# Mixer 2 with its heads' scores in pairs and its rows in column halves; the opening's loads and the window bias reordered

## The chip, the cores and the metric

One core of one Trainium2 chip runs the whole program. The metric is device time in microseconds (us) of that core, as the median of the runs shown. A profiled execution is a separate run; its span (first to last instruction) is what the trace divides up.

## What is computed

Two transformer-like blocks of two layers each, on a sequence of 256 tokens (two tiles of 128), width 1024, all in float32. Cut to its order:

```python
for l in range(2):                      # first block
    mod = silu(c) @ w_mod[l] + b_mod[l] # nine vectors of 1024: shifts, scales, gates
    x = x + 0.5 * g1 * swiglu(modulate(x, norm_g[l, 0], sh1, sc1), w_ffn1_gu[l], w_ffn1_down[l])
    x = x + g2 * (mixer_1(modulate(x, norm_g[l, 1], sh2, sc2)) @ w_out[l])
    #   mixer_1: 6 latent heads, 6 window heads with a relative-position bias, 4 stick-breaking heads
    x = x + 0.5 * g3 * swiglu(modulate(x, norm_g[l, 2], sh3, sc3), w_ffn2_gu[l], w_ffn2_down[l])
for l in range(2):                      # second block
    mod = silu(c_2) @ w_ada[l] + b_ada[l]
    q, k, v, g_sw, p_in, gates = split(h @ w_in[l])   # 11 strips of 512 columns
    ret = head_rmsnorm(retention(q, k, v))            # 8 heads, q and k of 64, v of 128
    ret_d = (silu(g_sw) * ret) @ w_ret_o[l]
    pool_d = (group_linear(causal_pool(p_in)) * pool_scale[l]) @ w_pool_o[l]
    merged = sigmoid(a_ret) * ret_d + sigmoid(a_pool) * pool_d
    x = x + g1 * (merged @ w_out[l])
    x = x + g2 * swiglu(modulate_2(rmsnorm(x, norm2[l]), sh2, sc2), w_ffn_in[l], w_ffn_out[l])
return rmsnorm(x, final_norm)
```

In retention, head by head, the scores q·k are multiplied by a fixed decay matrix and then applied to v.

## The kernel before

Each float32 operand is split into a high and a low part, and a product is made of three matmuls (high·high, high·low, low·high), lines 1776 to 1778. Weights stream in units of 128 x 1024. SP (SyncE's queue) loads a unit into one of six raw slots (`RING`), ScalarE writes its high part (`hi_static`, line 677), VectorE its low part (`lo_static`, line 1131), into seven slots (`PARTS`), and TensorE consumes it: 12 matmuls of 512 columns a unit in `strip_unit` and `rows_unit`. Semaphores count units: `w_loaded`, `hi_done`, `lo_done`, `mm_done`.

The order on each engine is written out by hand; nothing reorders it. There are eight phases: ffn, mixer 1, ffn, twice over, then mixer 2, ffn, twice over. Counted by `f`, the feed-forwards are f = 0 to 5; the mixers are m = 0, 1 of each kind.

The opening (lines 452 to 495, 809 to 834, 1333 to 1377, 1930 to 1943): SP loads 16 units of modulation weights (`mod_load`), then strip 0 of the first feed-forward. TensorE sums them (`mod_unit`), makes four of six `bias_pass`es between them, turns x (`x_turn`), and starts on strip 0 (`first_strip`, which wants for column pair u of a token tile both `lo_done` of unit u and `hlo_done`, counted by `x_low`). The rest of the constants, 768 KB, and five small gain vectors are loaded from ScalarE's queue behind the split of x (line 831), and TensorE waits for them before strip 1 (line 1943).

A feed-forward runs through 11 strips (`STRIPS`) of 256 gate and 256 up columns. In round b TensorE makes `gate_up` of strip b (4 units), in the middle of it the `turn` of strip b-1, then `down` of strip b-1 (2 units). VectorE splits weights, makes `gated` and `act_lo`, and adds up modulation units for later phases: `mod_slot(f, b)` says which ones in round b. Those units come through a ring of four slots (`MOD_RING`) that GpSimd's queue fills (line 426), each load waiting for the unit that had the slot. In a chunk of eight units the last is summed on TensorE (`mod_sum`), which also frees its slot.

The window bias is made in six passes: VectorE compares positions (`bias_reach`), TensorE multiplies (`bias_pass`, 64 small matmuls in banks 4 to 7), VectorE reduces (`bias_take`, four reductions). Passes 4 and 5 stand in mixer 1, m = 0, between the units of its second strip; `bias_mask` then applies scale and mask, in part in f = 0, round 3, in part in the mixer.

Mixer 2 (lines 2208 to 2338): strips 0 to 6 give q, k, v, the gate and the pool input; between strips 3 and 4 all four groups of transposes of q and k; after strip 6 the eight heads, one after another. For head i TensorE makes scores i, waits for VectorE's product with the decay, and makes values i-1. A head's q and k lie on partitions 0 to 63 or 64 to 127 by turns. Then strips 7 to 10, four groups of transposes of `ret`, the pooling matmuls, eight row units of `w_ret_o`, four of `w_pool_o`, eight of `w_out` behind `merged(0)` and `merged(1)`, which turn the two column halves of the merged rows. Banks of strips: `STRIP_BANKS`. The pool rows fill all four banks by rows first; only their last two units go by column half, and VectorE's merge of half 0 waits for `pool_half`.

## Time and profile before

| | us |
|---|---|
| median of three runs | 1874.15 |
| lowest, highest | 1869.9, 1875.66 |
| the profiled execution | 1882.45 |
| its span | 1880.6 |
| TensorE busy | 1813.6 (96%) |
| VectorE busy | 1340.4 (71%) |
| ScalarE busy | 920.3 (49%) |
| HBM traffic, mean | 233 GB/s |

Places in the span that are spoken of, in us from its start: opening 0 to 36, feed-forward f = 0 36 to 244, mixer 1 m = 0 244 to 364, m = 1 751 to 863, mixer 2 m = 0 1056 to 1273, m = 1 1474 to 1682. A row of a timeline gives start, length, engine, line, operation, result and operands, count, and in brackets the idle time before it and what ended it. A matmul's length covers its filling; the distance between starts is what it costs. In a table of windows, PEclk is the clock granted to TensorE as a share of its full 2.4 GHz: 1.00 is that level, 0.50 is 1.2 GHz.

### The profile page before, as it was taken

How to read it: one execution, taken by the hardware profiler on the slowest of the kernel's cores; microseconds unless marked ns; L12 is line 12 of the kernel's file. 1: busy time of each engine (PE TensorE's matmuls, PEld its weight loads, DVE VectorE, ACT ScalarE, POOL GpSimd, SP SyncE). 2: the span in 40 equal slices, each digit the busy share in tenths (PEclk: the TensorE clock that was granted, in tenths of full speed). 3: DMA queues.
4: the chain of work that ended last, by engine and by line, in shares of the span. 5: the costliest groups of instructions: out<-in, count | busy, mean ns of one | idle time of the engine just before them, and what ended most of it. 6: DMA issues, size and time to landing. Idle time of an engine off the chain costs nothing.

```text
span 1880.6 us, 24264 instructions
## 1 busy us (share of the span) xinstructions
PE 1813.6 (96%) x9140; PEld 1473.7 (78%) x9140; DVE 1340.4 (71%) x1825; ACT 920.3 (49%) x1507; POOL 177.3 (9%) x359
## 2 busy tenths in 40 slices
PE   6999989999999999999999999999999999999997
PEld 3778779788878887887888787877778787878886
DVE  6778777787878877768788765467777755477454
ACT  4343467743464445766433643446343644454344
POOL 3111010111101111011110000001111000000000
PEclk8999999999999999999999997999999999999999
DMA  9889733498959796517898652457898553456652
GB/s 343 317 306 339 286 101 113 157 318 300 329 207 342 274 339 220 169 46 252 301 331 312 210 198 90 164 177 258 311 343 308 190 189 135 152 188 237 213 201 79
DMA packets 241156, 439.49 MB, mean 234 GB/s; under 512 B 15168, under 2 KB 157328, under 8 KB 240912
## 3 DMA queue, kind: packets, MB, share of 16 engines
q1 hardware_dynamic: 205600, 311.09, 48.7%
q0 software_dynamic: 34016, 122.74, 17.2%
q10 hardware_dynamic: 1424, 4.12, 0.6%
q8 instruction: 72, 1.18, 0.2%
q14 instruction: 44, 0.36, 0.1%
HBM read 436.80 MB, written 1.09 MB: 233 GB/s over the span
## 4 chain that ended last, share of the span: by engine, by line
PE 79%; DVE 10%; DMA 5%; ACT 3%; issue 2%; SPq 0%; DVEq 0%; ACTq 0%
PE bank L1776 24%; PE bank L1778 23%; PE bank L1777 23%; DVE weights_lo L1131 5%; DMA arena<-in_w_mod 1%; PE bank L1966 1%; DMA arena<-in_w_ada 1%; DVE mod_acc L1152 1%; ACT weights_hi L677 1%; DMA weights_raw<-in_w_mod 1%; DVE x L1284 1%; DVE arena L1278 1%; PE bank L2252 1%; PE bank L1843 1%; DMA weights_raw<-in_w_ffn_in 1%
## 5 line engine op out<-in xcount | busy, mean ns | idle before, releaser
L1131 DVE TENSOR_TENSOR weights_lo<-weights_raw,weights_hi 128x1024 fp32r<-128x1024 f32 (+2 forms) x584 | 671.7, 1201 | 144.6 <-ACT weights_hi L677 143.8
L1776 PE MATMUL bank<-weights_hi,hT_hi 128*128 128x512 f32 (+1 forms) x1760 | 697.5, 396 | 16.6 <-DVE hT_lo L1248 6.6
L1778 PE MATMUL bank<-weights_hi,hT_lo 128*128 128x512 f32 (+1 forms) x1760 | 684.9, 389 | 0.0
L1777 PE MATMUL bank<-weights_lo,hT_hi 128*128 128x512 f32 (+1 forms) x1760 | 683.9, 389 | 0.0
L677 ACT ACTIVATE weights_hi<-weights_raw 128x1024 fp32r<-128x1024 f32 (+2 forms) x584 | 567.4, 1037 | 65.8 <-DMA weights_raw<-in_w_ffn_gu 22.1
L1776 PEld LDWEIGHTS bank<-weights_hi,hT_hi 128*128 128x128 f32 x1760 | 331.9, 189 | 87.7 <-DVE hT_lo L1248 6.8
L1778 PEld LDWEIGHTS bank<-weights_hi,hT_lo 128*128 128x128 f32 x1760 | 331.5, 188 | 68.3
L1777 PEld LDWEIGHTS bank<-weights_lo,hT_hi 128*128 128x128 f32 x1760 | 332.3, 189 | 62.5
L858 ACT ACTIVATE actT_hi<-bank 128x512 fp32r<-128x512 f32 x66 | 39.6, 599 | 502.6 <-PE bank L1966 502.6
L1152 DVE SCALAR_TENSOR_TENSOR mod_acc<-arena,silu_cond,mod_acc 128x1024 f32<-128x1024 f32 x184 | 236.2, 1284 | 50.0 <-DMA arena<-in_w_ada 17.5
L1776 PE MATMUL bank<-weights_hi,actT_hi 128*128 128x512 f32 (+2 forms) x552 | 218.0, 395 | 4.4 <-DVE weights_lo L1131 4.2
L1777 PE MATMUL bank<-weights_lo,actT_hi 128*128 128x512 f32 (+2 forms) x552 | 213.2, 386 | 0.0
L1778 PE MATMUL bank<-weights_hi,actT_lo 128*128 128x512 f32 (+2 forms) x552 | 213.1, 386 | 0.0
L1393 DVE TENSOR_TENSOR actT_lo<-bank,actT_hi 128x512 fp32r<-128x512 f32 x66 | 45.5, 690 | 125.3 <-ACT actT_hi L858 125.3
L1776 PEld LDWEIGHTS bank<-weights_hi,actT_hi 128*128 128x128 f32 x552 | 103.6, 188 | 38.4 <-issue 16.1
L1778 PEld LDWEIGHTS bank<-weights_hi,actT_lo 128*128 128x128 f32 x552 | 103.6, 188 | 21.3
L1777 PEld LDWEIGHTS bank<-weights_lo,actT_hi 128*128 128x128 f32 x552 | 103.7, 188 | 19.1
L426 POOL DMA_DIRECT2D arena<-in_w_mod x128 | 68.1, 533 | 419.5 <-DVE mod_acc L1152 221.1
L659 POOL TENSOR_TENSOR x<-x,arena 128x512 f32<-128x512 f32 x10 | 12.8, 1278 | 711.6 <-DVE arena L1278 711.6
L426 POOL DMA_DIRECT2D arena<-in_w_ada x96 | 50.9, 532 | 291.1 <-DVE mod_acc L1152 152.2
L853 ACT ACTIVATE arena<-bank 128x256 f32<-128x256 f32 x132 | 43.4, 381 | 63.2 <-PE bank L1778 63.2
L1388 DVE TENSOR_TENSOR arena<-arena,bank 128x256 f32<-128x256 f32 x132 | 49.3, 415 | 8.4 <-ACT arena L853 8.4
(274 smaller groups left out, 1259.0 us busy)
## 6 DMA issues: line engine op xcount, KB each, us to landing
weights_raw<-in_w_ffn_gu SPq DMA_DIRECT2D x176, 512.0 KB, 5.5
arena<-in_w_mod POOLq DMA_DIRECT2D x128, 512.0 KB, 6.7
weights_raw<-in_w_in SPq DMA_DIRECT2D x104, 512.0 KB, 4.8
arena<-in_w_ada POOLq DMA_DIRECT2D x96, 512.0 KB, 6.6
weights_raw<-in_w_ffn_down SPq DMA_DIRECT2D x88, 512.0 KB, 4.7
weights_raw<-in_w_ffn_in SPq DMA_DIRECT2D x88, 512.0 KB, 5.8
weights_raw<-in_w_ffn_out SPq DMA_DIRECT2D x44, 512.0 KB, 4.8
weights_raw<-in_w_out SPq DMA_DIRECT2D x32, 512.0 KB, 4.4
```

What stands on the lines that cost most here:

```text
L426: eng.dma_start(mod_tile(m), A[name][layer][k * P:(k + 1) * P, col:col + D]).then_inc(S(mod_sem(m)), 16)
L677: nc.scalar.activation(whi[:, n % PARTS, 0:width], raw[:, slot, 0:width], ACT.Copy).then_inc(S("hi_done"), 1)
L853: nc.scalar.activation(sg_t[:, t, :], bank[gu_banks(j)[t]][:, 0:256], ACT.Silu).then_inc(S("silu_done"), 1)
L858: nc.scalar.activation(ahi[:, j % 2].rearrange("p k n -> p (k n)"), bank[ATB][:, :], ACT.Copy)\
L1131: V.tensor_tensor(wlo[:, n % PARTS, 0:width], raw[:, n % RING, 0:width], whi[:, n % PARTS, 0:width].bitcast(F32), ALU.subtract).then_inc(S ...
L1152: V.scalar_tensor_tensor(acc, w, sc, acc, ALU.mult, ALU.add).then_inc(S("mod_used"), 1)
L1278: V.tensor_tensor(xn[:, t, c], bank[2 * t + h][:, :], gate_b[:, c], ALU.mult).then_inc(S("x_gated"), 1)
L1388: ins = V.tensor_tensor(act_t[:, t, :], sg_t[:, t, :], bank[gu_banks(j)[t]][:, 256:512], ALU.mult)
L1393: V.tensor_tensor(alo[:, j % 2].rearrange("p k n -> p (k n)"), bank[ATB][:, :], ahi[:, j % 2].rearrange("p k n -> p (k n)").bitcast(F32), ...
L1776: T.matmul(o, sh, wh, start=start, stop=False)
L1777: T.matmul(o, sh, wl, start=False, stop=False)
L1778: return T.matmul(o, sl, wh, start=False, stop=stop)
```

## The change

- Opening. SP loads 12 modulation units, then the first half of strip 0, then the other four, then the second half. ScalarE and VectorE split units 0 and 1 of it before the last modulation vector is stored; VectorE then splits units 2 and 3 behind `x_low(0)` and `x_low(1)`. The 768 KB of constants and the gains go from ScalarE's queue to SP's, ahead of strip 1; TensorE's wait for them moves into round 1.
- Window bias. Passes 4 and 5 move from mixer 1 into round 1 of f = 0, with buffers and banks 0 to 3 of their own; one mask over all 384 columns in round 3. Round 1 has no modulation units; its 42 are spread over rounds 2 to 10 (4, 5, 5, 4, 5, 5, 4, 5, 5).
- Mixer 2. Two groups of transposes of q and k, half of strip 4, the other two. Scores in pairs over banks 6, 7, 4, 5; the first pair before the last unit of strip 6, values 0 before that strip's copies. Half of the groups of `ret` are turned before strip 10 and go to the feed-forward's tiles. Pool rows go by column half throughout: 4 units of half 0, 3 of half 1, `merged(0)`, the last.

```diff
-    to = [min(len(units), max(4 * e, len(units) * e // 10)) for e in (b - 1, b)]
+    late = 1 if f == 0 else 0
+    to = [min(len(units), max(4 * e, len(units) * e // (10 - late))) for e in (max(b - 1 - late, 0), b - late)]
...
-STRIP_BANKS = [2 * (s % 3) for s in range(7)] + [4, 6, 0, 2]
+STRIP_BANKS = [0, 2, 4, 0, 2, 0, 4, 4, 6, 0, 2]
+STRIP_AFTER = {3: 0, 4: 1, 5: 3, 6: 2, 7: 6}
+SCORE_BANKS = (6, 7, 6, 7, 4, 5, 6, 7)
...
+            for m in range(MOD_AHEAD):
+                mod_load(sp, m)
+            sp.wait_ge(S("mod_read"), 6)
+            gu_strip(RING, phases[0][2]["gu"], 0, (0,))
+            for m in range(MOD_AHEAD, MOD_FIRST_UNITS):
+                mod_load(sp, m)
+            sp.wait_ge(S("mod_summed"), 1)
+            gu_strip(RING, phases[0][2]["gu"], 0, (1,))
...
-                        sp.wait_ge(S("mod_read"), 7)
-                        sp.wait_ge(S("mod_summed"), 1)
-                    gu_strip(n0, a["gu"], 0)
-                    if n0 == RING:
                         sp.wait_ge(S("mod_summed"), 2)
+                        sp.dma_start(con[:, C_FIRST:], A["con"][:, C_FIRST:]).then_inc(S("const_loaded"), 16)
+                        for dst, src in ((gq96[:, 0, :], "mla_q_norm"), (gq96[:, 1, :], "mla_k_norm"),
+                                         (gw64[:, 0, :], "swa_q_norm"), (gw64[:, 1, :], "swa_k_norm"), (sink[:, :], "sinks")):
+                            sp.dma_start(dst, A[src][0].partition_broadcast(P)).then_inc(S("gains_loaded"), 16)
+                    else:
...
                 hi_static(RING, SLOT)
+                hi_static(RING + 1, SLOT)
                 act.wait_ge(S("scale_ready"), 1)
                 x_hi(0)
                 x_hi(1)
...
+                        if s == 11:
+                            split_groups(4, tiles=[ahi[:, 0], ahi[:, 1]])
                         split_strip(s)
                     strip(10)
-                    split_groups(KD)
...
             bias_take(3)
+            lo_static(RING, SLOT)
+            lo_static(RING + 1, SLOT)
...
                         x_low(g)
-                        lo_static(n0 + g, SLOT)
+                        if g < 2:
+                            lo_static(n0 + 2 + g, SLOT)
...
+                    if f == 0:
+                        bias_reach(4)
+                        bias_reach(5)
                     gated(0)
                     for b in range(1, STRIPS):
                         c = n0 + 4 + 6 * (b - 1)
                         units(c + 2, c + 4)
                         mod_units(mod_slot(f, b))
+                        if f == 0 and b == 1:
+                            bias_take(4)
                         act_lo(b - 1)
-                        units(c + 4, c + 8)
+                        units(c + 4, c + 6)
+                        if f == 0 and b == 1:
+                            bias_take(5)
+                        units(c + 6, c + 8)
                         if b == STRIPS - 1 and after is not None:
                             units(end, end + 2)
                         gated(b)
                         if f == 0 and b == 3:
-                            bias_mask(0, 2 * P)
+                            bias_mask(0, 3 * P)
                         for chunk in mod_full(f, b):
                             mod_store(chunk)
...
+                            if s == 7:
+                                if m == 0:
+                                    dve.wait_ge(S("const2_loaded"), 16)
+                                probs(0)
+                                probs(1)
...
+                        if h == 0:
+                            lo_static(n0 + 60, SLOT)
+                        split_groups(KD // 2, banks=TRB_MERGED[2 * h:2 * h + 2], tiles=[(a[:, 0], a[:, 1]) if h == 0 else hT_tiles(w, 4) for a, w in ((ahi, hhi), (alo, hlo))])
+                        if h == 0:
+                            lo_static(n0 + 61, SLOT)
...
                         gate_up(c, 0, 2)
+                        if f == 0 and b == 1:
+                            bias_pass(4)
                         turn(b - 1)
-                        gate_up(c, 2, 4)
+                        gate_up(c, 2, 3)
+                        if f == 0 and b == 1:
+                            bias_pass(5)
+                            pe.wait_ge(S("const_loaded"), 32)
+                        gate_up(c, 3, 4)
+                        if f == 0 and b == 1:
+                            pe.wait_ge(S("bias_taken"), 6)
...
-                        if m == 0 and u in (0, 1):
-                            bias_pass(u + 4)
-                        if u == (2 if m == 0 else 1):
...
+                    def scores(i):
+                        r0 = 64 * (i % 2)
+                        q, k = qkT2[r0:r0 + 64, i // 2, :], qkT2[r0:r0 + 64, 4 + i // 2, :]
+                        b = bank[SCORE_BANKS[i]]
+                        if i >= 4:
+                            pe.wait_ge(S("ret_probs"), RH * m + i - 3)
+                        T.matmul(b[:, 0:SEQ], k[:, 0:P], q, start=True, stop=True)
+                        T.matmul(b[:, SEQ:384], k[:, P:SEQ], q[:, P:SEQ], start=True, stop=True).then_inc(S("ret_scores"), 1)
...
+                    qk_turn(0)
+                    qk_turn(1)
+                    strip(4, 0, 2)
+                    qk_turn(2)
+                    qk_turn(3)
+                    strip(4, 2, 4)
+                    strip(5)
...
+                    scores(0)
+                    scores(1)
+                    strip(6, 3, 4)
+                    copied(5)
+                    values(0)
+                    pe.wait_ge(S("ret_probs"), RH * m + 2)
+                    scores(2)
+                    scores(3)
+                    values(1)
+                    copied(6)
+                    scores(4)
+                    scores(5)
+                    values(2)
+                    values(3)
+                    scores(6)
+                    scores(7)
+                    for h in range(4, RH):
+                        values(h)
+                    for s in range(7, 10):
                         strip(s)
+                    copied(8)
                     pe.wait_ge(S("ret_ready"), m + 1)
-                    copied(8)
-                    transposes(ret, KD)
+                    transposes(ret, 4)
+                    strip(10)
+                    transposes(ret, KD, first=4)
...
-                    for u in range(2):
+
+                    def pool_rows(u, h):
                         n = n0 + 54 + u
-                        rows_unit(n % PARTS, n + 1, u, u == 0, False, hhi, hlo, first_bank=4)
-                    pe.wait_ge(S("lo_done"), n0 + 58)
-                    for h in range(2):
-                        for u in (2, 3):
-                            n = n0 + 54 + u
-                            wh = whi[:, n % PARTS, 512 * h:512 * (h + 1)]
-                            wl = wlo[:, n % PARTS, 512 * h:512 * (h + 1)]
-                            for t in range(NT):
-                                ins = products(bank[4 + 2 * t + h][:, :], u, t, wh, wl, False, u == 3)
                         if h == 0:
+                            pe.wait_ge(S("lo_done"), n + 1)
+                        wh = whi[:, n % PARTS, 512 * h:512 * (h + 1)]
+                        wl = wlo[:, n % PARTS, 512 * h:512 * (h + 1)]
+                        for t in range(NT):
+                            ins = products(bank[4 + 2 * t + h][:, :], u, t, wh, wl, u == 0, u == 3)
+                        if h == 1:
+                            ins.then_inc(S("mm_done"), 1)
+                        elif u == 3:
                             ins.then_inc(S("pool_half"), 1)
-                    ins.then_inc(S("mm_done"), 2)
...
+                    for u in range(4):
+                        pool_rows(u, 0)
+                    for u in range(3):
+                        pool_rows(u, 1)
                     merged(0)
                     split = tr[0] - 1
+                    pool_rows(3, 1)
                     for u in range(5):
...
```

## Rows read from the trace of the kernel before

**Rows 1.** The page's first part: busy us, share of the span, instructions.
```profile
PE 1813.6 (96%) x9140; PEld 1473.7 (78%) x9140; DVE 1340.4 (71%) x1825; ACT 920.3 (49%) x1507; POOL 177.3 (9%) x359
```

**Rows 2.** Waits of TensorE, whole span: us in total, times, longest us.
```profile
PE bank L2006 <- DVE arena L1452: 4.6, 2, 4.4
...
PE bank L2275 <- DVE hT_lo L1262: 2.5, 2, 1.2
...
PE bank L2325 <- DVE arena L1754: 2.1, 2, 1.0
PE bank L1776 <- DVE hT_lo L1262: 2.0, 2, 1.0
...
PE bank L2239 <- DVE arena L1683: 1.0, 2, 0.5
```

**Rows 3.** Timeline of TensorE, first feed-forward: strip 0, strip 1, first turn.
```profile
35.86 0.50 PE L1776 MATMUL bank<-weights_hi,hT_hi 128*128 128x512 f32 x1 [2.41 <-DVE weights_lo L1131]
...
52.45 0.80 PE L1776 MATMUL bank<-weights_hi,hT_hi 128*128 128x512 f32 x1 [4.20 <-DMA con<-in_con]
...
60.73 0.60 PE L1966 MATMUL bank<-con,arena 128*128 128x128 f32 x4
```

**Rows 4.** Windows: us, busy of PE, PEld, DVE, ACT, POOL, PEclk, DMA share, GB/s.
```profile
52.00:54.00 2.00, 1.54 (x4) 1.26 (x5) 1.88 (x3) 0.00 (x0) 0.00 (x0) 0.50 0.56 192
...
1140.00:1160.00 20.00, 20.00 (x69) 16.19 (x68) 5.12 (x15) 0.00 (x0) 0.00 (x0) 0.51 0.00 1
```

**Rows 5.** Timelines of ScalarE and VectorE in the opening.
```profile
36.69 1.04 ACT L677 ACTIVATE weights_hi<-weights_raw 128x1024 fp32r<-128x1024 f32 x1
...
34.24 0.43 DVE L1248 TENSOR_TENSOR hT_lo<-arena,hT_hi 128x256 fp32r<-128x256 f32 x1
```

**Rows 6.** The bias's instructions: duration ns minimum, median, maximum, first and last start.
```profile
L1174 DVE TENSOR_TENSOR arena<-arena x6: 2266/2292/2323, 7.9 to 256.0; 128x2048 bf16<-128x2048 f32 x6
...
L1182 DVE TENSOR_REDUCE window_bias<-bank x24: 442/448/460, 13.4 to 264.6; 128x96 f32<-128x288 f32 x24
```

**Rows 7.** Timelines of VectorE and TensorE, f = 0, round 4.
```profile
118.30 1.28 DVE L1152 SCALAR_TENSOR_TENSOR mod_acc<-arena,silu_cond,mod_acc 128x1024 f32<-128x1024 f32 x1 [4.22 <-DMA arena<-in_w_mod]
...
120.10 4.62 DVE L1131 TENSOR_TENSOR weights_lo<-weights_raw,weights_hi 128x1024 fp32r<-128x1024 f32 x4
...
121.47 0.47 PE L1776 MATMUL bank<-weights_hi,actT_hi 128*128 128x512 f32 x1 [1.87 <-DVE weights_lo L1131]
```

**Rows 8.** Timeline of TensorE, mixer 1: from strip 0 to the gate's turn, both layers.
```profile
243.57 0.47 PE L1776 MATMUL bank<-weights_hi,hT_hi 128*128 128x512 f32 x1 [0.19 <-DVE hT_lo L1248]
...
259.28 0.64 PE L1863 MATMUL bank<-arena 32*128 32x18 bf16 x64
...
277.01 0.27 PE L1888 MATMUL bank<-con,mod_cols 128*8 128x128 f32 x1
...
750.65 0.47 PE L1776 MATMUL bank<-weights_hi,hT_hi 128*128 128x512 f32 x1 [0.18 <-DVE hT_lo L1248]
...
775.54 0.27 PE L1888 MATMUL bank<-con,mod_cols 128*8 128x128 f32 x1
```

**Rows 9.** Timeline of TensorE, mixer 2: scores L2252, values L2260, next strip L1776.
```profile
1137.96 0.71 PE L2252 MATMUL bank<-arena 64*128 64x256 f32 x4 [0.83 <-ACT arena L1061]
...
1139.63 0.49 PE L2260 MATMUL bank<-arena 128*128 128x128 f32 x2 [0.74 <-DVE arena L1695]
...
1160.56 0.57 PE L1776 MATMUL bank<-weights_hi,hT_hi 128*128 128x512 f32 x1
...
1558.41 0.70 PE L2252 MATMUL bank<-arena 64*128 64x256 f32 x2
...
1559.26 0.49 PE L2260 MATMUL bank<-arena 128*128 128x128 f32 x2
...
1568.60 0.49 PE L2260 MATMUL bank<-arena 128*128 128x128 f32 x2
...
1569.29 0.48 PE L1776 MATMUL bank<-weights_hi,hT_hi 128*128 128x512 f32 x1
```

129 lines of the change are left out of this document (52 added, 77 removed).

## The prediction

> **What bounds the kernel now.** I read the page's busy shares first: TensorE is busy 1813.6 of 1880.6 us [rows 1], so it is the bound, and a change can only gain in its 67 us of idleness or where a matmul runs slower than elsewhere. Second, TensorE's waits over the whole span, to name that idleness: each line of them stands in one or two places only, and four recur once per layer of mixer 2 [rows 2]. Third, the granted clock in windows: 1.00 nearly everywhere, but 0.50 behind the wait for the constants and 0.51 for 20.0 us in the heads of mixer 2, m = 0 [rows 4]. Fourth, the same stage in both layers, side by side in the timeline: what the one has and the other hasn't is what can go.
>
> **The base.** The sum is made against the profiled execution: 1882.45 us, a span of 1880.6 and 1.85 around it. That lies 8.3 us above the median, 1874.15. The slow heads of m = 0 cost about 9 us (below), so I suspect that most timed runs lack them. Then part of my gain below exists only against the profiled run. The prediction is that of a run without slow heads, so it needs no correction; if the timed runs had them too, the answer would lie lower by up to 8.
>
> **Opening.** Before, VectorE finishes `x_low(0)` at 34.24 + 0.43 = 34.7 [rows 5] and then splits unit 0, so TensorE starts at 35.86 [rows 3]. With units 0 and 1 split ahead it can start at 34.7. But 1 MB of weights now goes ahead of the last four modulation units; they may land later by up to its own time, and I put 0.5 us on the chain (0 to 1.5). TensorE's second column pair wants `x_low(1)`, and that now stands behind the split of unit 2, whose high part ScalarE makes only after two x groups and a scaling: before that ended at 36.69 + 1.04 = 37.7 [rows 5], with one more unit ahead of it; now about 36.7 + 0.5. Then a split, 4.62/4 = 1.2 [rows 7], and 0.4 for `x_low(1)`: 38.8. So TensorE does one unit (1.4 us), waits 2.3, and finds the rest in about the old order. Strip 0, over at 48.25 before (52.45 less 4.20), is over at about 49.1: **+0.8**. The early units buy nothing.
>
> The wait for the constants goes: **-4.2** [rows 3]. Behind it the clock is at 0.50 [rows 4], and the 24 matmuls from 52.45 to 60.73 take 8.28 us, where 24 at 0.227 take 5.45: **-2.8**. The load isn't cheaper, only needed later: SP issues it at some 32, TensorE asks for it in the middle of round 1, beyond 58. Behind it on SP's queue stand strip 1's loads, later by the six issues, some 3.5 us: they are issued at 35.5 to 38. A load that lands 6 to 9 us later is split by 47.7, before TensorE's 49.1. If that cover were gone each microsecond would count in full.
>
> What the Trainium skill says here: in "Trainium Kernel Development and Optimization", Key Constraints, DMAs from the SP, ACT and POOL queues run on the same 16 engines and interleave, so another queue saves issue time alone. By that the constants still take their share from strip 1's loads wherever they are issued, and nothing is gained from the move in itself; my sum takes no gain from it either.
>
> **Bias passes.** They cost TensorE 0.64 us each [rows 8]: **+1.3** in round 1, in place of the same in mixer 1. VectorE gets 2 x 2.29 and 2 x 4 x 0.45 = 8.2 us [rows 6] instead of four modulation units (4.9). `gated(0)` is queued behind both `bias_reach`es: splits to 48.9, reaches to 53.5, gate to 54.2; TensorE comes to pass 4 at 49.1 + 5.5 = 54.6. Just hidden. `bias_take(5)` stands behind two splits and ends at some 62.6, where TensorE arrives at 61.7: **+0.9**. Sum of opening and round 1: **-4.0**, from -7 (no late landing) to +2.
>
> **Five units a round.** Before, rounds 5 and 10 had five. In round 4 a burst crosses the unit that TensorE sums, needs a fifth slot of a ring of four, and VectorE waits 4.22 us for the load; TensorE then stands 1.87 [rows 7]. Now six rounds have five units, three of them with the crossing. VectorE has slack: six splits 7.2, gate 0.75, `act_lo` 0.7, five units 6.4, together 15.1 of TensorE's 16.8 (six units of 2.73 and a turn). In round 3 the mask stands ahead of the store that round 4's gate turn wants, and round 4's burst starts as late as before with a unit more: 1.3 more. The others I take as hidden to 0.3 each, round 10 as it was: **+1.2**, 0 to +7.
>
> **Mixer 1, m = 0.** From strip 0 to the gate's turn it takes 277.01 - 243.57 = 33.4 us, in m = 1, without bias work, 775.54 - 750.65 = 24.9 [rows 8]. The difference holds both passes, the wait of 4.4 for the latent rows that VectorE makes late (of 4.6 in [rows 2]), and a low clock behind it. What is late next is what is late in m = 1, a wait of 0.2. **-8.5**, -7 to -9.
>
> **Mixer 2.** Three things per layer. (1) The gaps: 0.5 at the q, k transposes (half of strip 4 now hides the copies), 1.25 ahead of the pooling (strip 10 does), 1.05 and 1.0 at `merged(0)` [rows 2]. For the last two: half 0 of the pool rows is now complete after four half units, 5.5 us; VectorE's merge needs 2.5 and is over at 8.1; TensorE has 4.1 us of half 1 and arrives at 9.6. Then 1.4 us of half 1 cover the split of the first group. All four go: **-3.8**.
>
> (2) The heads. In m = 1 strip 7 starts at 1569.29. Scores of one head take 1559.26 - 1558.41 = 0.85, values 0.86 with the change to scores behind them, 0.69 at the end where values or the strip follow. The one pair of scores that stands together takes, in m = 0, 1137.96 to 1139.63 less the wait of 0.74: 0.93, hardly more than one [rows 9]. From the end of strip 6 to the first values it is 2.50 in m = 0 (0.83 of it a wait), and the second scores follow 0.86 on; so in m = 1 strip 6 ended at 1555.05, and the heads take 14.2 us. Now: eight values of 0.69 to 0.86 and four pairs of 0.93, one of them inside strip 6: 9.2 to 10.6, taken 9.9. The waits: VectorE's products take 0.65, between values h-2 and h there are always other values or a pair of 0.7 to 0.9, and the copies of strip 6 are passed by values 0, a pair and values 1. **-4.3**, -3.6 to -5.
>
> (3) The clock. In m = 0 the same stretch takes 1160.56 - 1137.13 = 23.4, at 0.51 [rows 4, 9]; that is 9.2 more than in m = 1, where the instructions are the same. The fall comes just after two waits and among small matmuls. Without the waits and with 4 us less of it, I take it that the clock holds: **-9.2**.
>
> Two layers: -16.2 - 9.2 = -25.4.
>
> **A rule for and against the pairs.** "TensorEngine Tiling (Array Packing)", Key Properties, in the Trainium skill says that tiles on other rows run in parallel, which the 0.93 bears out, and that a change of tiling mode drains TensorE; the trace agrees in so far as values cost 0.86 ahead of scores and 0.69 ahead of their like. By this rule the pairs gain twice, as there are fewer changes; with 0.69 throughout, the heads would be at my lower end.
>
> **Sum.** -4.0 + 1.2 - 8.5 - 25.4 = -36.7; 1882.45 - 36.7 = 1845.7, so **1846 us**.
>
> **Rivals.**
> - The clock falls in the heads of one layer again, in half the runs or more. Against it: no waits left ahead; for it: nothing distinguishes m = 0 from m = 1 now. Some 9.9 us of work at half speed: 1846 + 9 = **1855**.
> - The fifth unit is paid each time: six stalls of 1.9 instead of the 5.3 that I count, +6, and with the unit itself (1.3) +14: **1852 to 1860**, say 1855. For it: [rows 7]; against: bursts that crossed in other rounds were hidden.
> - The pairs don't overlap, because the second waits on something of the first (the change doesn't do what it says): 0.77 for each of eight pairs, +6: **1852**. Against it stands the one pair of [rows 9].
> - The other side: VectorE becomes the bound of the first feed-forward. Its 15.1 us a round and an unhidden wait w for a modulation load, in each of nine rounds, against 16.8. It is slower than before from w = 1.7 + 37/9 = 5.8 us on; now 4.2 was seen once [rows 7]. With heavier traffic, w = 6.5: 9 x 4.8 = 43, **1888**.
>
> **Numbers.** My forecast has 0.60 (its own range 1838 to 1851), the clock 0.15, the fifth unit 0.13, no overlap 0.05, something better than the forecast (timed runs with slow heads before as well) 0.04, the other side 0.03. The range is 1837 to 1859. A measurement of this kernel tells 0.3%, 5.6 us, from no change: faster by more 0.95, within 0.02, slower 0.03.
>
> **What would show it.** In the changed kernel's trace: no wait for the constants, and granted clock 1.00 from strip 0 to round 4; a wait of some 2.3 us ahead of strip 0's second pair; about 0.9 ahead of `down` in round 1; mixer 1's stretch of [rows 8] within 1 us in both layers; none of the last four waits of [rows 2]; strip 6 to strip 7 in 9 to 10 us in both layers at 1.00. I am wrong if the clock is below 1.00 in the heads, if waits of TensorE for line 1131 appear in rounds 3, 6 and 9, or if strip 1 waits for its weights.

## The result and the profile of the changed kernel

The changed kernel takes 1846.32 us (median of four runs, 1843.98 to 1850.63), the kernel before 1874.91 (four runs, 1869.9 to 1876.04): ratio of the means 0.9855, 95% interval 0.983 to 0.9881. The forecast was 1846.0. The profiled execution took 1846.53 us, its span 1844.7, against 1882.45 and 1880.6 before.

TensorE's waits over the whole span, against [rows 2] (total, times, longest):

```profile
...
PE bank L1797 <- DVE hT_lo L1259: 8.8, 20, 2.1
PE bank L1988 <- DVE arena L1402: 5.3, 5, 2.6
...
PE bank L1797 <- DVE weights_lo L1142: 2.5, 3, 1.4
PE bank L1928 <- ACT arena L722: 2.4, 2, 1.3
...
PE bank L1864 <- DVE mod_acc L1163: 1.2, 1, 1.2
PE bank L1911 <- DVE mod_cols L1178: 1.1, 1, 1.1
PE bank L2034 <- DVE arena L1463: 0.4, 2, 0.2
```

The wait for the latent rows (L2034, 4.6 before) is down to 0.4, that for the constants is gone, and so are the four of mixer 2. New are those in the first feed-forward: the gate's turn (L1911), a modulation sum (L1864), and more ahead of the last turns (L1988).

The windows of TensorE, against [rows 4] (us, PE busy, granted clock, DMA share, GB/s):

```profile
20.00:40.00 20.00, 15.27 (x222) 0.67 0.87 303
40.00:60.00 20.00, 18.32 (x142) 1.00 0.91 323
1120.00:1140.00 20.00, 19.89 (x126) 1.00 0.41 138
1420.00:1440.00 20.00, 18.04 (x87) 0.91 0.79 284
```

The heads of mixer 2, m = 0, which stood at 0.51 before, are at 1.00. The low clock behind the constants' wait is gone. The stretch from 20 to 40 us is at 0.67. In the kernel before it had 0.74, with the DMA engines busier:

```profile
20.00:40.00 20.00, 16.47 (x232) 0.74 0.94 325
```

Where the time went, by the ten stages in their order. A stage begins with the first matmul on `hT_hi` behind the transposes of x. I give the kernel before twice, since a second profile of it (e_before, below) looks different:

| stage | before, as profiled | before, again | changed |
|---|---|---|---|
| to mixer 1, m = 0 | 243.57 | 241.25 | 243.45 |
| mixer 1, m = 0 | 118.47 | 118.46 | 108.93 |
| f = 1 | 195.19 | 195.24 | 195.19 |
| f = 2 | 193.42 | 193.41 | 193.43 |
| mixer 1, m = 1 | 110.18 | 109.07 | 108.97 |
| f = 3 | 195.47 | 195.42 | 195.17 |
| mixer 2, m = 0 | 215.32 | 205.90 | 196.85 |
| f = 4 | 202.62 | 206.90 | 205.16 |
| mixer 2, m = 1 | 205.99 | 205.92 | 197.04 |
| f = 5 to the end | 200.37 | 200.53 | 200.51 |
| span | 1880.6 | 1872.1 | 1844.7 |

Three stages carry the gain: mixer 1, m = 0 with 9.5, and mixer 2 with 9.0 and 8.9 (against the second profile; the first has 9.4 us more in mixer 2, m = 0). Between the second profile and the changed kernel lie 27.4 us, between the first and it 35.9. The opening and the first feed-forward together gave nothing: 0.1 against the first profile, and 2.2 longer than the second. The opening in the changed kernel, TensorE and then VectorE, against [rows 3, 5]:

```profile
30.52 1.08 PE L1873 MATMUL bank<-arena,silu_cond 128*32 128x256 f32 x8 [0.63 <-DMA arena<-in_w_mod]
...
41.22 0.47 PE L1797 MATMUL bank<-weights_hi,hT_hi 128*128 128x512 f32 x1 [2.11 <-DVE hT_lo L1259]
43.30 0.47 PE L1797 MATMUL bank<-weights_hi,hT_hi 128*128 128x512 f32 x1 [0.46 <-DVE hT_lo L1259]
...
57.69 0.66 PE L1988 MATMUL bank<-con,arena 128*128 128x128 f32 x4
```

```profile
34.25 0.42 DVE L1174 TENSOR_TENSOR arena<-bank,con 128x256 f32<-128x256 f32 x1 [1.49 <-PE bank L1873]
...
36.90 0.43 DVE L1259 TENSOR_TENSOR hT_lo<-arena,hT_hi 128x256 fp32r<-128x256 f32 x1
39.51 1.23 DVE L1142 TENSOR_TENSOR weights_lo<-weights_raw,weights_hi 128x1024 fp32r<-128x1024 f32 x1 [2.18 <-ACT weights_hi L690]
```

The 2.11 us ahead of the second column pair is there, as it had to be. But VectorE gets the last modulation sum only at 34.25 us, and `x_low(0)` runs at 36.90 where it ran at 34.24 before. The first turn comes at 57.69 instead of 60.73 (58.62 in the second profile of the kernel before).

### The profile page after: what moved, and what is told of

Same layout as the page of the kernel before. It is cut to its first block, busy times and chain, and to the rows that moved or that the text cites. A ratio compares the mean times of both kernels' runs of the same rounds, so it can differ in the third digit from the quotient of the medians.

```text
span 1844.7 us, 24265 instructions
## 1 busy us (share of the span) xinstructions
PE 1788.9 (97%) x9140; PEld 1456.1 (79%) x9140; DVE 1340.6 (73%) x1824; ACT 920.4 (50%) x1507; POOL 176.4 (10%) x359
## 4 chain that ended last, share of the span: by engine, by line
PE 78%; DVE 9%; DMA 7%; ACT 3%; issue 2%; SPq 0%; DVEq 0%; POOL 0%; ACTq 0%
PE bank L1797 24%; PE bank L1799 23%; PE bank L1798 23%; DVE weights_lo L1142 5%; DMA arena<-in_w_mod 2%; PE bank L1988 1%; DMA weights_raw<-in_w_ffn_gu 1%; DMA weights_raw<-in_w_mod 1%; DMA arena<-in_w_ada 1%; DVE mod_acc L1163 1%; ACT weights_hi L690 1%; ACT arena L731 1%; DMA weights_raw<-in_w_ffn_in 1%; DVE x L1295 1%; PE bank L1864 1%
## 5 line engine op out<-in xcount | busy, mean ns | idle before, releaser
L1797 PE MATMUL bank<-weights_hi,hT_hi 128*128 128x512 f32 (+2 forms) x1696 | 669.8, 395 | 10.8 <-DVE hT_lo L1259 8.8
L1799 PE MATMUL bank<-weights_hi,hT_lo 128*128 128x512 f32 (+2 forms) x1696 | 658.3, 388 | 0.0
L1798 PE MATMUL bank<-weights_lo,hT_hi 128*128 128x512 f32 (+2 forms) x1696 | 657.1, 387 | 0.0
L1797 PEld LDWEIGHTS bank<-weights_hi,hT_hi 128*128 128x128 f32 x1696 | 318.5, 188 | 77.8 <-issue 7.3
L1799 PEld LDWEIGHTS bank<-weights_hi,hT_lo 128*128 128x128 f32 x1696 | 318.3, 188 | 65.3
L1798 PEld LDWEIGHTS bank<-weights_lo,hT_hi 128*128 128x128 f32 x1696 | 318.9, 188 | 59.5
L1797 PE MATMUL bank<-weights_hi,actT_hi 128*128 128x512 f32 (+1 forms) x616 | 243.9, 396 | 2.8 <-DVE weights_lo L1142 2.5
L1798 PE MATMUL bank<-weights_lo,actT_hi 128*128 128x512 f32 (+1 forms) x616 | 238.8, 388 | 0.0
L1799 PE MATMUL bank<-weights_hi,actT_lo 128*128 128x512 f32 (+1 forms) x616 | 238.7, 388 | 0.0
L1799 PEld LDWEIGHTS bank<-weights_hi,actT_lo 128*128 128x128 f32 x616 | 116.1, 188 | 24.0
```

What stands on the lines that cost most here:

```text
L1797: T.matmul(o, sh, wh, start=start, stop=False)
L1798: T.matmul(o, sh, wl, start=False, stop=False)
L1799: return T.matmul(o, sl, wh, start=False, stop=stop)
```

## The experiments

Times of different series are not finely comparable: beside my kernels the median of the kernel before lay between 1872.09 and 1874.95 us. I therefore go by the stages of the traces wherever a difference is small.

### Is the slow stretch in the heads always there?

The kernel before, unchanged.

> The kernel before, unchanged, profiled a second time. Theory (the base of the prediction): the half clock in mixer 2's heads of m = 0 belongs to some executions only, so this one shows a granted clock of 1.00 from 1140 to 1160 us with probability of about two in three, and then a span of 1880.6 - 9.2 = about 1871.5 and a time near 1873, the median of the timed runs. Rival A: the half clock stands in every execution at that place (0.50 to 0.55 again, m = 0 some 9 us longer than m = 1) and the profiled run is long for another reason. Rival B: the low clock wanders: m = 0 is at 1.00 and another stage is slow.

Measured: 1873.88 us, span 1872.1. The window that stood at 0.51 in [rows 4]:

```profile
1140.00:1160.00 20.00, 20.00 (x104) 1.00 0.22 64
```

In four series beside my kernels the kernel before ran 48 times: 39 times between 1869.3 and 1877, nine times between 1880 and 1889.3 at a granted clock of 0.982 to 0.989 (4 of 13, 3 of 7, 1 of 17, 1 of 11). The first profile belonged to the second group; of the other nine only the time and the mean clock are known, and that they were slow in the heads too is inferred from these. So the 9.2 us of half clock belong to some executions, as the theory said; if the inference holds, to about one in five.

### Where did the opening's gain go?

e_con is the kernel before with one wait moved:

```diff
                     first_strip(n0, strip_banks, 1)
-                    pe.wait_ge(S("const_loaded"), 32)
...
-                        gate_up(c, 2, 4)
+                        gate_up(c, 2, 3)
+                        if f == 0 and b == 1:
+                            pe.wait_ge(S("const_loaded"), 32)
+                        gate_up(c, 3, 4)
```

> The kernel before with one edit: TensorE's wait for the constants stands in the middle of round 1 of the first feed-forward instead of ahead of it; their load stays on ScalarE's queue. Theory (the prediction's step): the 4.2 us wait goes and the half clock behind it with it, 7.0 us in all: first turn at 60.73 - 7.0 = 53.7 us. Rival: the clock falls there whatever the wait (it is low at 20 to 60 us for the small matmuls of the opening), then 4.2 us alone, first turn at 56.5. Second rival: strip 1's weights are late too and a wait for them takes the place of part of it, first turn at 57 or later.

Measured: 1874.89 us against 1874.95, ratio 0.9999 (0.9972 to 1.0025). The first turn comes at 54.15: 6.6 us earlier than in the first profile of the kernel before, 4.5 earlier than in the second. But one round later (TensorE, then VectorE):

```profile
80.91 0.77 PE L1776 MATMUL bank<-weights_hi,actT_hi 128*128 128x512 f32 x1 [2.91 <-DVE weights_lo L1131]
81.47 0.63 PE L1777 MATMUL bank<-weights_lo,actT_hi 128*128 128x512 f32 x1
81.90 0.63 PE L1778 MATMUL bank<-weights_hi,actT_lo 128*128 128x512 f32 x1
```

```profile
78.28 0.75 DVE L1149 TENSOR_SCALAR mod_acc<-arena,silu_cond 128x1024 f32<-128x1024 f32 x1 [3.12 <-DMA arena<-in_w_mod]
78.95 0.68 DVE L1393 TENSOR_TENSOR actT_lo<-bank,actT_hi 128x512 fp32r<-128x512 f32 x1
79.55 4.62 DVE L1131 TENSOR_TENSOR weights_lo<-weights_raw,weights_hi 128x1024 fp32r<-128x1024 f32 x4
```

VectorE waits 3.12 us for a modulation unit, its splits stand behind that, TensorE waits 2.91, and the clock falls (matmuls 0.43 apart instead of 0.23): this round takes 23.7 us instead of 18.05. Mixer 1 starts at 242.26, between the 243.57 and 241.25 of the two profiles of before. The first theory gave the right size at the first turn, and at the end of the stage nothing of it can be told.

The two medians hide something: in either kernel the executions fall into two groups, and e_con had five of ten in the upper one where the kernel before had four of thirteen. The median of the lower groups is 1871.02 against 1872.82. So up to 1.8 us may have arrived, and the equal medians come in part from the mix.

e_modsfirst is the changed kernel with the opening's order undone:

```diff
-            for m in range(MOD_AHEAD):
-                mod_load(sp, m)
-            sp.wait_ge(S("mod_read"), 6)
-            gu_strip(RING, phases[0][2]["gu"], 0, (0,))
-            for m in range(MOD_AHEAD, MOD_FIRST_UNITS):
+            for m in range(MOD_FIRST_UNITS):
                 mod_load(sp, m)
+            sp.wait_ge(S("mod_read"), 7)
             sp.wait_ge(S("mod_summed"), 1)
-            gu_strip(RING, phases[0][2]["gu"], 0, (1,))
+            gu_strip(RING, phases[0][2]["gu"], 0)
```

with the splits of the first units between the x groups as in the kernel before.

> The changed kernel with the opening's order undone: all 16 modulation units are loaded ahead of the first weights again, and the splits of the first units stand between the x groups as before. The constants stay on SyncE's queue, the bias passes in round 1. Theory (from the two traces): the 1 MB of early weights pushes the last modulation units back by 2.2 to 2.7 us and all behind them; so the first turn comes at 60.73 - 7.0 + 0.6 = 54.4 us instead of 57.69, and the whole is 3.3 us shorter. Rival: the delay comes from the constants' load in SyncE's queue ahead of strip 1, then the modulation is summed at 31.5 again but the first turn stays at 56 to 58 and the whole gains under 1 us. Second rival: the gain of the opening is given back in round 2 to 4, where VectorE has no slack: turns earlier, the end of the first feed-forward at 243.4 as now.

Measured: 1845.58 us (1844.1 to 1846.98), 0.7 below the changed kernel and not to be told from it. The first sum and the first turn:

```profile
30.41 0.42 DVE L1171 TENSOR_TENSOR arena<-bank,con 128x256 f32<-128x256 f32 x1 [1.42 <-PE bank L1867]
```

```profile
54.46 0.66 PE L1982 MATMUL bank<-con,arena 128*128 128x128 f32 x4
```

Between these two profiles the early megabyte costs 34.25 - 30.41 = 3.8 us at the sum, 36.90 - 34.11 = 2.8 at `x_low(0)`, which in e_modsfirst waits for ScalarE instead, and 3.2 at the first turn. Executions scatter here: with the modulation loaded first the sum came at 30.37 to 31.55 us in six profiles.

The second rival holds for the rest: mixer 1 starts at 243.31, as in the changed kernel. But that start is a coarse measure. Five profiles have the same code up to there (the changed kernel, e_gaps, e_heads, e_samerow, e_mix2), and in them it lies at 243.45, 244.13, 244.55, 245.20 and 246.39. Against their median e_modsfirst is 1.2 us early, so of 3.2 us something between nothing and 1.2 arrived.

e_half is e_modsfirst with 512 of 1024 columns of each modulation unit loaded in the first feed-forward:

```diff
-            eng.dma_start(mod_tile(m), A[name][layer][k * P:(k + 1) * P, col:col + D]).then_inc(S(mod_sem(m)), 16)
+            w = D // 2 if MOD_FIRST_UNITS <= m < 64 else D
+            eng.dma_start(mod_tile(m)[:, 0:w], A[name][layer][k * P:(k + 1) * P, col:col + w]).then_inc(S(mod_sem(m)), 16)
```

> The kernel of e_modsfirst (opening's order undone, first turn at 54.46 us) with half of the bytes of the modulation units of the first feed-forward left out (512 of 1024 columns loaded, VectorE's work unchanged). e_modsfirst started 3.2 us earlier than the changed kernel and yet ended the first feed-forward at 243.31 as that one did (243.45). Theory (the loads of the modulation units set the pace: VectorE waits for them, TensorE stands at the gate's turn, at the sums and at the last turn): with half the bytes the waits at 116, 170 and 231 us go or shrink and the first strip of mixer 1 starts 3 to 6 us earlier, at 238 to 240. Rival (VectorE's own work is the bound, above all the mask and five units a round): the waits stay, the start at 243 +- 0.7. Second rival: the clock, low around 220 to 240 us in e_modsfirst (0.91), takes the 3 us; then this run gains only where that window is back at 1.00.

Measured: 1837.65 us (1836.39 to 1839.55). First turn at 54.12, mixer 1 at 234.47 instead of 243.31: 8.8 us, more than expected, and 9.0 below the lowest of the five starts above. TensorE's waits from 45 us to the end of the last turn, e_modsfirst first, then e_half:

```profile
PE bank L1982 <- DVE arena L1396: 3.3, 1, 3.3
PE bank L1858 <- DMA arena<-in_w_mod: 2.4, 2, 1.3
PE bank L1905 <- DVE mod_cols L1175: 1.5, 1, 1.5
```

```profile
PE bank L1792 <- DVE weights_lo L1140: 0.5, 1, 0.5
PE bank L1906 <- DVE mod_cols L1176: 0.3, 1, 0.3
```

VectorE's waits for these units, from 45 us to the last turn, e_modsfirst first, then e_half:

```profile
DVE mod_acc L1160 <- DMA arena<-in_w_mod: 13.2, 9, 3.6
DVE mod_acc L1157 <- DMA arena<-in_w_mod: 11.6, 3, 4.5
```

```profile
DVE mod_acc L1158 <- DMA arena<-in_w_mod: 10.3, 3, 4.1
DVE mod_acc L1161 <- DMA arena<-in_w_mod: 5.9, 5, 2.5
```

VectorE's work is the same in both; only the bytes differ. So the transfers hold the first feed-forward back, and VectorE's own work alone doesn't. Of the 8.8 us, 7.2 - 0.8 = 6.4 are the waits in these fences; the rest is for the most part the clock, which is at 0.91 from 220 to 240 us in e_modsfirst (20 x 0.09 = 1.8 us) and not low there in e_half.

### The bias passes and the fifth unit

e_biasmix puts both passes, their reaches, takes and the last mask back into mixer 1, m = 0, and spreads the modulation units of f = 0 over ten rounds:

```diff
-    late = 1 if f == 0 else 0
+    late = 0
...
-                        if f == 0 and b == 1:
-                            bias_pass(4)
...
+                        if m == 0 and u in (0, 1):
+                            bias_pass(u + 4)
```

> The changed kernel with both bias passes, their masks and reaches back in mixer 1 of m = 0, and the modulation units over ten rounds of the first feed-forward again; all else as changed. Theory (the prediction's terms): mixer 1 of m = 0 is 8.5 us longer (9.5 by the two traces), with a wait of some 4.4 us for the latent rows; the first feed-forward is 3.4 us shorter (1.3 for the passes, 0.9 for the wait, 1.2 for the fifth unit); in all +5 to +6.5. Rival A: the move's cost in the first feed-forward is smaller than that (the passes fall into its slack), then +8 to +9.5. Rival B: the latent rows are late for something else that the change took away too (the opening), then mixer 1 of m = 0 stays within 1 us of m = 1.

Measured: 1853.28 us (1848.99 to 1856.47), +7.0. Mixer 1, m = 0 takes 117.76 us, +8.8, and the old wait for the latent rows is back:

```profile
PE bank L2034 <- DVE arena L1466: 4.4, 1, 4.4
```

The first feed-forward doesn't get shorter by the 3.4 us of the theory: mixer 1 starts at 243.95, within the 243.45 to 246.39 of the five profiles. By stages that is rival A; the time, +7.0, lies between the theory's 5 to 6.5 and the rival's 8 to 9.5, while the two profiled executions differ by 8.6.

e_ten keeps the passes in round 1 and only sets `late = 0`.

> The changed kernel with the modulation units of the first feed-forward over ten rounds again (four of them in round 1, beside the bias passes' work of VectorE). Theory (the loads of these units set the pace, not their number in a round): an earlier start of the loads' use takes more from the waits at rounds 4 to 10 than round 1 loses (VectorE has 21.8 us of work there against TensorE's 18.1, so up to +3.7 in round 1); the end of the first feed-forward at 242 to 244. Rival A (the prediction's term: the fifth unit costs 1.2 us and round 1 has no room): round 1 to 2 is longer by 3.7 and later rounds give back 1.2, the end at 246. Rival B: everything is hidden by the slack that the late loads leave anyway, and the end is at 239 to 241.

Measured: 1849.76 us (1846.9 to 1851.02), +3.4, with the two series overlapping; mixer 1 starts at 246.93, only 0.5 above the highest of the five. The loss is plain within the round. From first to second turn it takes 21.98 us instead of 17.64, since TensorE waits for the first `bias_take`, which stands behind four modulation units:

```profile
64.15 0.65 PE L1886 MATMUL bank<-arena 32*128 32x18 bf16 x64 [2.80 <-DVE window_bias L1193]
```

Rival A fits for round 1: VectorE has no room there, and 4.3 us are lost. So the passes are free only if the units leave that round. The price of the five units themselves doesn't show; that the units come late in either case would explain it, but no run separates the two.

### Mixer 2

e_heads sets the heads back to the single order:

```diff
-SCORE_BANKS = (6, 7, 6, 7, 4, 5, 6, 7)
+SCORE_BANKS = (6, 7, 6, 7, 6, 7, 6, 7)
...
-                    strip(6, 0, 3)
...
-                    scores(0)
-                    scores(1)
-                    strip(6, 3, 4)
-                    copied(5)
-                    values(0)
...
+                    strip(6)
+                    copied(5)
+                    for i in range(RH + 1):
+                        if i < RH:
+                            scores(i)
+                        if i >= 1:
+                            values(i - 1)
+                    copied(6)
```

> The changed kernel with the heads of mixer 2 in the single order again: all after strip 6, score banks 6 and 7 in turn, scores i and values i-1 alternating; the rest of mixer 2 as changed. Theory (the prediction's term): 14.2 us instead of 9.7 a layer at full clock, two layers +9. And the half clock, which the kernel before showed in mixer 2's heads in some executions (the time then 1880 to 1886 instead of 1870 to 1877), comes back in part of the executions: some near 1846 + 9 = 1855, some near 1864. Rival A: the single order is cheaper than 14.2 now that its waits have other cover, +6 or less. Rival B: the half clock belonged to the waits and gaps around the heads, which stay away here: then all executions lie together near 1855, and so does the granted clock (0.991 or above).

Measured: 1854.97 us (1852.61 to 1855.34), +8.6; by stages +3.5 and +3.4, the rest in f = 0 and behind, where nothing was edited. From the first scores at 1126.73 to strip 7 at 1140.17 it takes 13.4 us, of it 0.77 a wait. In the changed kernel it is 0.86 for the pair inside strip 6 and 8.82 from values 0 to strip 7:

```profile
1126.23 0.38 PE L2283 MATMUL bank<-arena 128*128 128x128 f32 x2
...
1126.99 0.71 PE L2275 MATMUL bank<-arena 64*128 64x256 f32 x4
1127.53 0.40 PE L2276 MATMUL bank<-arena 64*128 64x128 f32 x4
1127.85 0.49 PE L2283 MATMUL bank<-arena 128*128 128x128 f32 x2
...
1135.05 0.48 PE L1797 MATMUL bank<-weights_hi,hT_hi 128*128 128x512 f32 x1
```

Rival B on the clock: the four executions lie together, none has the half clock. With one execution in five, four without it are no surprise, so this doesn't decide. The size lies between the theory's +9 and rival A's +6: the stages give 6.9.

e_samerow reads both heads of a pair from the same rows:

```diff
-                        r0 = 64 * (i % 2)
+                        r0 = 64 * (i // 2 % 2)
```

> The changed kernel with both heads of a pair read from the same 64 rows (so the scores are those of another head for half of the heads; the amount of work is the same). Theory (the pair overlaps because its two heads stand on different rows of the array): a pair takes about 1.6 us instead of 0.86, four pairs and two layers, +5 to +6 us, heads 8.82 + 3 x 0.75 = 11.1 us from the first values to strip 7. Rival A (a pair is cheap because two scores share one change between kinds of matmul, not because of the rows): +0 to 1 us. Rival B: VectorE's products of 0.65 become late with the pair's second half, or are hidden even better; then the difference per pair is not the same in all four.

Measured: 1853.35 us (1852.6 to 1854.42), +7.0; by stages +2.6 and +2.6, the rest elsewhere. A pair now runs one head after the other:

```profile
1129.74 0.70 PE L2275 MATMUL bank<-arena 64*128 64x256 f32 x2
1130.27 0.38 PE L2276 MATMUL bank<-arena 64*128 64x128 f32 x2
1130.49 0.59 PE L2275 MATMUL bank<-arena 64*128 64x256 f32 x2
1130.93 0.38 PE L2276 MATMUL bank<-arena 64*128 64x128 f32 x2
1131.24 0.49 PE L2283 MATMUL bank<-arena 128*128 128x128 f32 x2
```

1.50 us against 0.86, in each of the three pairs alike: the rows are the cause, to 0.64 us a pair.

e_gaps undoes TensorE's order at three places:

```diff
-                    for u in range(4):
-                        pool_rows(u, 0)
-                    for u in range(3):
-                        pool_rows(u, 1)
+                    for u in (0, 1):
+                        pool_rows(u, 0)
+                        pool_rows(u, 1)
+                    for u in (2, 3):
+                        pool_rows(u, 0)
+                    for u in (2, 3):
+                        pool_rows(u, 1)
                     merged(0)
```

and likewise `strip(10)` ahead of `transposes(ret, 4)` and all `qk_turn`s ahead of `strip(4)`.

> The changed kernel with TensorE's order of three places in mixer 2 undone: the four q, k transposes in one block, strip 10 ahead of the retention's transposes, and the pool rows half by half only from the third unit on, with the first merged transposes behind all of them. Theory (the prediction's gaps term): the waits return, 0.5 + 1.25 + 1.05 + 1.0 = 3.8 us a layer, 7.6 us in all. Rival A: part of them stays away, because the splits of the transposed groups now lie in tiles of their own (this edit leaves that in), then 1 to 5 us. Rival B: the clock falls behind the returned waits, and the cost is above 9 us.

Measured: 1858.19 us (1857.3 to 1858.41), +11.9; by stages +4.6 and +4.0, the rest in f = 0 and f = 4. The waits in mixer 2, m = 0:

```profile
PE bank L1797 <- DVE actT_lo L1273: 1.0, 1, 1.0
PE bank L1797 <- ACT arena L1065: 1.0, 1, 1.0
PE bank L2326 <- DVE actT_lo L1273: 0.7, 1, 0.7
...
PE bank L2266 <- DVE arena L1707: 0.5, 1, 0.5
```

They sum to 3.2; the stage is longer by 4.6, so the theory's 3.8 is a little low for the whole. What the other 1.4 us are isn't shown.

e_mix2 undoes both.

> The changed kernel with both of mixer 2's edits undone together (the heads of e_heads and the three places of e_gaps). Singly they cost +3.5 us a layer (e_heads) and +4.3 us a layer (e_gaps), and no execution of either showed the half clock. Theory (the half clock in the heads needs the waits ahead and the long row of small matmuls together): now part of the executions, about a third as in the kernel before, is 8 to 11 us longer than the rest, with a granted clock lower by 0.004 or more; the rest lies at 1846 + 2 x 7.8 = 1862. Rival A: the half clock came from something else in the kernel before (the bias work or the opening); then all executions lie near 1862 within 3 us. Rival B: the two edits overlap in their effect, then the fast executions lie at 1857 or at 1866.

Measured: 1863.18 us, twelve executions from 1861.02 to 1868.2; by stages +7.9 and +7.5. The two edits add up. The half clock doesn't show in any of the twelve, but in this series the kernel before had it only once in 17, so this doesn't tell the theory from rival A.

### Towards a better version

> Towards a better version: e_modsfirst (all modulation units loaded ahead of the first weights), the mask moved from round 3 to round 6, so that the store for the gate's turn isn't behind it, only four modulation units in the last two rounds of the first feed-forward, and in the first and fifth feed-forward only one unit of the next stage split ahead of the last gate instead of two. Theory (waits of TensorE in e_modsfirst's first feed-forward: 1.46 at the gate's turn, 1.27 and 1.16 at the sums, 3.28 at the last turn, and 2.0 at the last turn of the fifth): the gate's wait goes (-1.5), the last turns' shrink by 1.2 to 2.5 each, 3 to 5 us in all, about 1842. Rival A: the loads set the pace, so that what is gained at 104 us is waited for again at 117 and 231, under 1 us in all, about 1845. Rival B: the unit that is now split behind the gate delays the next stage by what the gate gains; then only the first 1.5 us remain.

Measured: 1847.32 us (1846.56 to 1848.99). Rival A, and worse: TensorE waits 6.5 us for late splits between 45 and 247 us, and mixer 1 starts at 246.94. Of the edits the six rounds in a row with five units are the likely cause; they weren't tried alone. The wait at the gate's turn went, as expected. The fifth feed-forward alone took 203.18 us, 2 less.

So e_last takes that edit alone:

```diff
-                            units(end, end + 2)
+                            units(end, end + (1 if f in (0, 4) else 2))
...
-                    boundary(phase[0], end, after, 2 if kind == "ffn" else 0)
+                    boundary(phase[0], end, after, 1 if f in (0, 4) else 2)
```

> Towards a better version, one edit alone: the changed kernel with one unit of the next stage split ahead of the last gate instead of two, in the first and fifth feed-forward. In the changed kernel TensorE waits 2.61 us ahead of the last turn of the first and 1.97 us ahead of that of the fifth, and behind the second the clock is low (0.91 from 1420 to 1440 us); in eleven profiles so far the fifth feed-forward had the low clock wherever that wait was 1.97 us or more (nine of them), and not at 1.02 and 1.24. Theory: the waits shrink by 1.2 us, to 1.4 and 0.8, the low clock of the fifth goes, its stage takes 203.2 us as in e_best instead of 205.2, the first feed-forward ends 0.5 to 1 us earlier: in all -2.5 to -3, about 1843.5. Rival A: the moved split delays the stage that follows by what it gives (two places), and only the clock's part of 1 us remains: 1845.5. Rival B: the loads of the modulation units come later by chance and the wait is 2 us again: no difference, 1846.3.

Measured: 1845.0 us, six executions from 1843.96 to 1846.34. That is 1.3 below the changed kernel, but the two series overlap, and the kernel before was 2.8 lower beside it (1872.09 against 1874.91): a gain of the whole is not shown. The last turn of the fifth feed-forward and the window, against 1.97 us and 0.91 in the changed kernel:

```profile
1434.57 0.66 PE L1988 MATMUL bank<-con,arena 128*128 128x128 f32 x4 [0.85 <-DVE arena L1402]
```

```profile
1420.00:1440.00 20.00, 19.12 (x98) 1.00 0.75 262
```

This stage takes 203.17 us, the 2.0 less that was expected, against 205.10 to 207.21 in the nine profiles of the changed kernel and its variants without this edit: in this stage the gain is shown. In the first feed-forward the wait is 2.14, and another for a late unit (2.06 at 119.40) brought a low clock: nothing gained there. The count in the expectation was wrong: of the thirteen profiles until then eleven had a wait of 1.97 us or more ahead of that turn; ten of these had the low clock behind it, and e_con, with 2.29, hadn't.

## Why the prediction came out right, and where it didn't

- **The base.** Right. A second profile of the kernel before has the heads at 1.00 and a time of 1873.88; taking the 9.2 us off the profiled run and not correcting again was the right way. Most timed runs lack the slow heads, as I suspected (39 of 48, by their times). The forecast of a time of 1846 thus stood; as a gain, 9.2 of the 36.7 us exist only against the first profile.
- **Opening, -4.0 with round 1.** Wrong in size. The wait for the constants and the low clock behind it are worth what I gave them: e_modsfirst's first turn is 6.3 us before that of the kernel before (4.2 + 2.8 - 0.64 = 6.4). The step that failed is "they may land later by up to its own time, and I put 0.5 us on the chain (0 to 1.5)". The last sum came 2.7 later than in the kernel before (34.25 against 31.55). The window from 20 to 40 us had the size: 1.05 MB take 3.5 us at the 303 GB/s of the changed kernel and 3.2 at the 325 of the kernel before, whose DMA share of 0.94 left little to hide it in. So the first turn gained 3.0, not 5.5, and only 0.9 against the second profile.
- **A second miss behind it.** I let the opening's gain run through to the end. e_con and e_modsfirst show that most or all of it is waited for again within the first feed-forward, and e_half that the bytes of the modulation units set that stage's pace. The rival of the other side had this mechanism (VectorE waiting for such a load), only as a loss, not as what swallows a gain. The second profile of before has the DMA share, as the profile gives it, at 0.66 to 1.04 in each 20 us from 40 to 220 us; the first shows VectorE's wait of 4.22 us in [rows 7]. The sentence of the Trainium skill that I weighed ("Trainium Kernel Development and Optimization", Key Constraints: the queues run on the same 16 engines and interleave) speaks of loads from different queues, and I used it for the constants alone. The early weights stand on the same queue, SP's, as the modulation units behind them; of that the sentence says nothing. What such bytes cost is measured here alone: 2.8 us at `x_low(0)` and 3.2 at the first turn.
- **Five units a round, +1.2; passes, +1.3 and +0.9.** The working of the first doesn't add up: 1.3 for round 4 and 0.3 for each of four others are 2.5, of which the sum took 1.2; the 5.3 in the rival isn't derived either. None of the three shows at the start of mixer 1 (e_biasmix, 0.5 us between the two, where equal code scatters by 2.9). But the order is not free to choose: e_ten loses 4.3 us in round 1. The 0.9 ahead of `down` in round 1, named as a sign, is not in the trace, and no wait for a late split stands in rounds 3, 6 or 9, the sign of being wrong. The foreseen wait at the gate's turn in round 4, behind the mask, is there with 1.1 us, and those for the late unit with 1.2 and 0.7.
- **Mixer 1, m = 0, -8.5.** -9.5 by the traces, -8.8 by e_biasmix. The stretch of [rows 8] takes 268.16 - 243.45 = 24.7 us now, 8.7 less, and 24.8 in m = 1: the sign that I named. e_biasmix brings the wait and the low clock behind it back (0.83 from 260 to 280 us, 1.00 in the changed kernel), so the cause is shown. The rest lies further on, where both profiles of the kernel before had the clock at 0.91 (320 to 340 us).
- **Mixer 2, gaps -3.8 and heads -4.3 a layer.** The sum, -8.1, was -9.0 and -8.9. Gaps 4.0 to 4.6, heads 3.4 to 3.5 by the undoings, 7.5 to 7.9 together, so both edits are shown as causes; what is missing to 9.0 is for the most part the wait of 0.83 us that the kernel before has ahead of its first scores [rows 9], for ScalarE's copy of strip 6. It was inside my 14.2 (13.4 and the wait), and e_heads doesn't have it; that this is for its changed `STRIP_BANKS` wasn't tried. The heads take 9.68 us in both layers, predicted 9.9, 4.5 less than 14.2. The 3.8 for the gaps was a little low.
- **The rule for the pairs.** "TensorEngine Tiling (Array Packing)", Key Properties, in the Trainium skill: tiles on other rows run in parallel. e_samerow shows it as 0.86 against 1.50. The second half of my rule was read wrong: the 0.69 stood ahead of a strip, not of other values. With fewer changes values take 0.78 on average, (8.82 - 3 x 0.86) / 8, between my two bounds.
- **The clock in the heads, -9.2.** Right in number against the profiled run. Of 54 executions of the changed kernel and its ten variants none is 8 us above the fastest of its own kind, and the eleven profiles have the heads of both layers at 1.00. But in about four of five executions of the kernel before there was nothing to gain here, and e_heads, e_gaps and e_mix2 didn't bring the half clock back. So my reason, that the clock holds without the waits and with a shorter stretch, isn't shown, and why it stays away is open.
- **f = 4 and mixer 1, m = 1.** I hadn't spoken of either; they differ by +2.5 and -1.2 from the first profile and by -1.7 and -0.1 from the second. For f = 4 it is the scatter of executions: waits of 1.0 to 3.2 us ahead of its last turn, and in most profiles a low clock behind them. Mixer 1, m = 1 took 110.18 and 109.94 in two profiles of the old order (before, e_con) and 108.97 to 109.34 in all others; why isn't known.
- **The total.** -35.9 between the spans, -36.7 forecast. That it fits so well is luck, because misses cancel: the opening gave 2.7 less, mixer 1 and mixer 2 gave 1.0 and 2.0 more, and the scatter of f = 4 and mixer 1, m = 1 adds 2.5 - 1.2. Against the second profile, with the 9.2 us left out on both sides, -27.4 stand against -27.5, and the opening with the first feed-forward missed by 5.0 (2.2 longer instead of 2.8 shorter), made up by mixer 1, mixer 2 and the scatter of f = 4.

## What to carry to other kernels

Here, at a DMA share of 0.87 to 0.94, bytes moved ahead cost about their whole transfer time (3.5 us) to what was behind them (2.7 to 3.8), and time gained ahead of a stage that waits for transfers was for the most part waited for again inside it. So price an opening by the next such wait, not by the one that goes. Half the bytes, with the work unchanged, is the experiment that shows such a pace. Profile the kernel before twice before a difference between stages is put down to a change, and collect the same stage from all profiles that share its code: that gives its scatter.

## What the runs showed of the hardware

- In some executions of the same program a stage runs at the half clock (0.51 over 20 us, 9 us longer), in others not. One profile shows it and one doesn't; by time and mean clock alone, 9 of 48 executions of the kernel before had it, and 5 of 10 of e_con in a series where the kernel before had 4 of 13.
- Low clocks in the feed-forwards came behind waits ahead of a last turn and for late splits or units; matmuls of 512 columns are then 0.43 us apart (1.2 GHz) instead of 0.23 (2.4 GHz), for 2 to 5 us. It isn't the wait's length alone: of 23 waits of 1.89 to 3.28 us ahead of the last turn of the first and fifth feed-forward, over the fourteen profiles, 16 had the low clock behind them and seven hadn't, among them 2.61 in the changed kernel's first and 2.89 in that of e_gaps.
- The opening and first feed-forward, where waits for transfers are many, differ by up to 2.9 us between executions of the same code (mixer 1 starts at 243.45 to 246.39 in five profiles, and at 241.25 and 243.57 in two of the kernel before); f = 1 and f = 2 repeat to 0.1 us in all fourteen.
- Scores of two heads of 64 rows each take 0.86 us when the heads stand on different rows of the array and 1.50 on the same (e_samerow).
